# A decoder layer on one core: down biases join the sums late, gate and up biases are loaded once

## The reference

```
logits = hx @ w_router + b_router;  comb = softmax weights of the top 4 of 32
for each expert e:                       # w_gate_up[e] 1024x2048, w_down[e] 1024x1024
    gu  = hx @ w_gate_up[e] + b_gate_up[e]
    act = min(gate, 7) * sigmoid(1.702 * gate) * (clip(up, -7, 7) + 1)
    acc += comb[:, e] * (act @ w_down[e] + b_down[e])
y = LayerNorm(alpha * hx + acc) * ln2_g + ln2_b
```

## Time and profile before

| | |
|---|---|
| time, median of 3 runs | 1180.72 us (1180.72 to 1181.76) |
| the profiled execution, its own time | 1180.89 us |
| its span, first to last instruction | 1178.8 us |
| TensorE busy | 1121.9 us, 95% of the span |
| VectorE busy | 289.7 us, 25% |
| ScalarE busy | 203.8 us, 17% |
| HBM read | 450.19 MB |
| mean granted clock of TensorE | 0.990 |

### The profile page before, as it was taken

How to read it: one execution, slowest core, us unless ns; L and a number is a source line. 1 busy time by engine, 2 the same in 40 slices (tenths; PEclk the granted TensorE clock), 3 DMA queues, 4 the chain that set the end, 5 groups by cost and what they waited for, 6 DMA issues and landing times.

```text
span 1178.8 us, 14219 instructions
## 1 busy us (share of the span) xinstructions
PE 1121.9 (95%) x5374; PEld 457.7 (39%) x5375; DVE 289.7 (25%) x707; ACT 203.8 (17%) x479; POOL 30.1 (3%) x65
## 2 busy tenths in 40 slices
PE   7999999899999999999999999999999999999986
PEld 6876764533333333333332323233333333333322
DVE  1543747602121211303030303030303030303113
ACT  1322412402020202021111111111111111111111
POOL 0110111000000000000000000000000000000001
PEclk9999999899999999999999999999999999999998
DMA  9857779668999999999999999999999999999992
GB/s 361 324 197 254 269 270 384 257 263 341 423 428 427 427 428 428 429 428 428 428 428 428 428 428 428 428 427 428 429 428 428 428 428 428 428 428 428 413 424 108
DMA packets 83399, 454.21 MB, mean 385 GB/s; under 512 B 7147, under 2 KB 20099, under 8 KB 36132
## 3 DMA queue, kind: packets, MB, share of 16 engines
q1 hardware_dynamic: 80866, 440.97, 90.5%
q0 software_dynamic: 1728, 10.75, 2.5%
q10 hardware_dynamic: 770, 2.03, 0.4%
HBM read 450.19 MB, written 11.93 MB: 392 GB/s over the span
## 4 chain that ended last, share of the span: by engine, by line
PE 65%; DMA 26%; SPq 5%; ACT 2%; DVE 1%; issue 1%
DMA ring<-in_w_gate_up 23%; PE bank L1083 19%; PE bank L1125 15%; PE bank L968 5%; PE bank L664 5%; PE bank L687 5%; SPq L445 3%; PE bank L851 3%; PE bank L690 2%; DMA ring<-in_w_down 2%; PE bank L1150 2%; PE bank L964 1%; SPq L455 1%; PE bank L804 1%; ACT xtok L1313 1%; ACT actT L1313 1%
## 5 line engine op out<-in xcount | busy, mean ns | idle before, releaser
L1083 PE MATMUL bank<-ring,xg 128*64 128x512 f32 x1904 | 422.8, 597 | 23.8 <-DMA ring<-in_w_gate_up 23.8
L1083 PEld LDWEIGHTS bank<-ring,xg 128*64 128x64 f32 x1904 | 132.0, 137 | 304.8 <-issue 252.3
L1125 PE MATMUL bank<-ring,actT 128*64 128x512 f32 x960 | 215.9, 597 | 3.8 <-ACT actT L1313 3.8
L1930 DVE TENSOR_TENSOR acc<-acc,bank 128x512 f32<-128x512 f32 x60 | 41.2, 687 | 509.3 <-PE bank L1150 509.3
L1458 ACT ACTIVATE sig<-gate 128x256 f32<-128x256 f32 x64 | 26.7, 416 | 545.6 <-DVE gate L1912 545.6
L1125 PEld LDWEIGHTS bank<-ring,actT 128*64 128x64 f32 x960 | 66.6, 137 | 121.5 <-issue 118.7
L1912 DVE TENSOR_SCALAR gate<-bank 128x256 f32<-128x256 f32 x64 | 26.8, 419 | 179.0 <-PE bank L1083 157.3
L687 PE MATMUL bank<-xT,wblk 128*128 128x288 f32 x256 | 67.1, 417 | 1.4 <-DMA wblk<-in_w_in 1.4
L1450 ACT ACTIVATE xg<-bank,small 128x128 f32<-128x128 f32 x128 | 48.1, 458 | 99.1 <-PE bank L664 99.1
L968 PE MATMUL bank<-hx,pick 128*128 128x512 f32 x128 | 61.6, 626 | 0.0
L1150 PE MATMUL bank<-ybuf,spread 128*128 128x512 f32 x120 | 58.3, 618 | 0.0
(11 more groups left out here) (245 smaller groups left out, 716.8 us busy)
## 6 DMA issues: line engine op xcount, KB each, us to landing
ring<-in_w_gate_up SPq DMA_DIRECT2D x119, 2048.0 KB, 29.2
ring<-in_w_down SPq DMA_DIRECT2D x63, 2048.0 KB, 31.5
ring<-in_w_gate_up SPq DMA_DIRECT2D x16, 1024.0 KB, 18.3
wblk<-in_w_in SPq DMA_DIRECT2D x12, 1024.0 KB, 7.4
kring<-in_cache_k_moba SPq DMA_DIRECT2D x16, 256.0 KB, 5.2
vring<-in_cache_v_moba SPq DMA_DIRECT2D x16, 256.0 KB, 5.0
out<-in_state_k_win POOLq DMA_DIRECT2D x8, 512.0 KB, 4.3
out<-in_state_v_win POOLq DMA_DIRECT2D x8, 512.0 KB, 4.9
```

The lines of the kernel that those rows point to most:

```text
L1083: ins = nc.tensor.matmul(bank[n][64 * e:64 * e + 64, :], xg[:, k, 64 * e:64 * e + 64], w[:, 2048 * e + 512 * n:2048 * e + 512 * n + 512], ...
L1125: ins = nc.tensor.matmul(bank[4 + half][64 * e:64 * e + 64, :], actT[:, j, 64 * e:64 * e + 64], w[:, at:at + 512], start=(j == 0), stop=(j ...
L1930: V.tensor_tensor(o, o, new, ALU.add).then_inc(S.added, 1)
```

## The change

- The gate and up biases of all 32 experts are loaded once, in four DMAs of 32 rows, to partitions 32n to 32n+31 of `bias_rows`. For each pair VectorE makes a matrix `sel` of 32 rows (four times, one in each group of partitions) from a 32-column identity in the constants: columns of ones where row = expert. `begin_gate_up` multiplies with it, over 32 rows in place of two, and waits for it. SP's waits and loads for each pair's biases go.
- The down biases are no longer added in pair 0. In pair 14's down stage (`finish_with_biases`) TensorE turns the combination weights behind the first down unit, makes two bias products behind the second, and two more and the samples' part behind the third. They go to banks 0 to 3, which are free there. The samples' part makes first the four matmuls with the identity and then the four with `combT`. VectorE adds them to the totals before it adds pair 14's mix, and the last gate-up waits for that.
- ScalarE copies the turned weights ahead of its copies of pair 15's slots.
- `bdn` goes to partitions 64 to 96 of hx's third tile and `combT` to the same partitions beside `samp_x`, since both must live until pair 14. `acc_s` starts from zero.
- On SP the wait for the scaled sums and the load of ln2_g move ahead of unit 9 of pair 0.

```
-        def load_bias(p):
-            src = b_gate_up[0, pair_of(p), :].rearrange("e (n c) -> e n c", c=512)
-            for n in range(4):
-                sp.dma_start(bias_rows[32 * n:32 * n + 2, :], src[:, n, :]).then_inc(S.bias_in, 16)
-
-        load_bias(0)
+        for n in range(4):
+            sp.dma_start(bias_rows[E * n:E * n + E, :], b_gate_up[0, :, 512 * n:512 * n + 512]).then_inc(S.bias_in, 16)
...
-        sp.dma_start(bdn[0:E, :], b_down[0]).then_inc(S.bdn_in, 16)
-        sp.dma_start(bdn[E:E + 1, :], ln1_b[0:1, :]).then_inc(S.bdn_in, 16)
+        sp.dma_start(hx[64:64 + E, 2, :], b_down[0]).then_inc(S.bdn_in, 16)
+        sp.dma_start(hx[64 + E:65 + E, 2, :], ln1_b[0:1, :]).then_inc(S.bdn_in, 16)
...
-        def next_bias(i):
-            sp.wait_ge(S.bias_used, i + 1)
-            load_bias(i + 1)
-
+        sp.wait_ge(S.added, 5)
+        sp.dma_start(ln_g[:, :], ln2_g[0:1, :].broadcast_to([128, D])).then_inc(S.ln2_in, 16)
         load_units(0, 0, range(9, UNITS))
-        sp.wait_ge(S.sums_scaled, 6)
-        sp.dma_start(ln_g[:, :], ln2_g[0:1, :].broadcast_to([128, D])).then_inc(S.ln2_in, 16)
-        next_bias(0)
         load_units(0, 1, range(UNITS))
         with sp.Fori(1, PAIRS // 2 - 1) as m:
-            next_bias(m * 2 - 1)
             load_units(m, 0, range(UNITS))
-            next_bias(m * 2)
             load_units(m, 1, range(UNITS))
...
         def add_sample_biases():
-            pe.wait_ge(S.added, 3)
             pe.wait_ge(S.sums_scaled, 2)
+            pe.wait_ge(S.bias_added, 2)
             for q in range(4):
                 r, c = slice(NS * q, NS * q + NS), slice(256 * q, 256 * q + 256)
-                nc.tensor.matmul(bank[4][r, 0:256], ident[0:NS, 0:NS], samp_x[:, c], start=True, stop=True,
+                nc.tensor.matmul(bank[0][r, 0:256], ident[0:NS, 0:NS], samp_x[:, c], start=True, stop=True,
                                  tile_position=(0, NS * q))
-                ins = nc.tensor.matmul(bank[4][r, 256:512], combT[:, SEQ:T], bdn[:, c], start=True, stop=True,
-                                       tile_position=(0, NS * q))
-            ins.then_inc(S.spread_down, 1)
+            for q in range(4):
+                r, c = slice(NS * q, NS * q + NS), slice(256 * q, 256 * q + 256)
+                ins = nc.tensor.matmul(bank[1][r, 0:256], combT[:, SEQ:T], bdn[:, c], start=True, stop=True,
+                                       tile_position=(64, NS * q))
+            ins.then_inc(S.bias_sums, 1)
...
-            pe.wait_ge(S.bias_in, i * 64 + 64)
+            pe.wait_ge(S.bias_in, 64)
+            pe.wait_ge(S.selected, i + 1)
             for n in range(4):
-                r = slice(32 * n, 32 * n + 2)
-                ins = nc.tensor.matmul(bank[n][:, :], keep[r, C_SEL:C_SEL + 2 * SLOTS], bias_rows[r, :], start=True,
-                                       stop=False, tile_position=(32 * n, 0))
+                r = slice(E * n, E * n + E)
+                ins = nc.tensor.matmul(bank[n][:, :], sel[r, :], bias_rows[r, :], start=True, stop=False,
+                                       tile_position=(E * n, 0))
...
+        def finish_with_biases(i, m, odd):
+
+            def first_slots():
+                turn_slots(i + 1, 0)
+                turn_comb()
+
+            def other_slots():
+                pe.wait_ge(S.actT_ready, i * 2 + 2)
+                turn_slots(i + 1, 1)
+                for j in range(2):
+                    add_biases(j)
+
+            def other_biases():
+                for j in range(2, 4):
+                    add_biases(j)
+                add_sample_biases()
+
+            gather(i + 1, i * 2)
+            turn_weights(i, i * 2 + 3)
+            turn_act(i, i * 2 + 4)
+            down(i, m, odd, {0: first_slots, 1: other_slots, 2: other_biases})
...
-        gate_up(0, 0, 0, {1: turn_comb, 4: lambda: add_biases(0), 5: lambda: add_biases(1), 6: add_sample_biases})
+        gate_up(0, 0, 0)
...
         def last_gate_up(between):
 
+            pe.wait_ge(S.bias_added, 5)
             begin_gate_up(last)
...
+        def select(i, p):
+
+            if not isinstance(i, int) or i > 0:
+                dve.wait_ge(S.bias_used, i)
+            V.tensor_copy(sel[:, :].rearrange("p (e s) -> p e s", e=2),
+                          eye[:, pair_of(p)].unsqueeze(2).broadcast_to([128, 2, SLOTS])).then_inc(S.selected, 1)
...
-        start_sums()
+        select(1, 1)
         swiglu(0)
         with dve.Fori(0, PAIRS - 2) as i:
             weigh_slots(i + 1, i + 1)
             add_mixed(i)
             pick_slots(i + 2, i + 2, 0)
+            select(i + 2, i + 2)
             swiglu(i + 1)
         weigh_slots(PAIRS - 1, PAIRS - 1)
+        dve.wait_ge(S.added, 5 * PAIRS - 5)
+        add_biases()
+        dve.wait_ge(S.bias_added, 5)
         add_mixed(PAIRS - 2)
```

More of the change, by code:

```diff
@@ L44 @@
 C_ID, C_TRI, C_ONE, C_IOTA = 0, 128, 256, 384
-C_SEL = C_IOTA + CHUNKS * SLOTS
-C_HEAD = C_SEL + 2 * SLOTS
+C_EYE = C_IOTA + CHUNKS * SLOTS
+C_HEAD = C_EYE + E
 C_MEAN = C_HEAD + H
@@ L69, in constant_tables @@
     keep[:, C_ONE:C_ONE + 128] = 1
-    keep[:, C_IOTA:C_SEL] = np.arange(CHUNKS * SLOTS)
-    for n in range(4):
-        for e in range(2):
-            keep[32 * n + e, C_SEL + e * SLOTS:C_SEL + (e + 1) * SLOTS] = 1
+    keep[:, C_IOTA:C_EYE] = np.arange(CHUNKS * SLOTS)
+    keep[p, C_EYE + p % E] = 1
     keep[p, C_HEAD + p // DS % H] = 1
@@ L149, in build_layer @@
     bias_rows = place("bias_rows", [128, 512])
+    sel = place("sel", [128, 2 * SLOTS])
     share_at = cursor[0]
@@ L167, in build_layer @@
     ln_gs, ln_bs = place("ln_gs", [128, 256]), place("ln_bs", [128, 256])
+    late_at = cursor[0]
     samp_x = place("samp_x", [NS, D])
+    bdn = hx[64:64 + E + 1, 2, :]
+    combT = place("combT", [128, T], at=late_at)[64:64 + E + 1, :]
     wrt = place("wrt", [128, KC, E], at=share_at)
@@ L1188, in _ @@
         last = PAIRS - 1
-        finish(last - 1, last // 2, 0, last // 2, following=False)
+        finish_with_biases(last - 1, last // 2, 0)
         def last_gate_up(between):
+            pe.wait_ge(S.bias_added, 5)
             begin_gate_up(last)
@@ L1476, in _ @@
         take_slots(0)
-        act.wait_ge(S.comb_turned, 1)
-        copy(combT[0:E, :], bank[4][0:E, 0:T]).then_inc(S.combT_ready, 1)
         sigmoids(0)
@@ L1486, in between_pairs, with take_comb @@
             take_down(i)
+        def take_comb():
+            act.wait_ge(S.comb_turned, 1)
+            copy(combT[0:E, :], bank[3][0:E, 0:T]).then_inc(S.combT_ready, 1)
         with act.Fori(0, PAIRS - 2) as i:
@@ L1490, in _ @@
             sigmoids(i + 1)
-        between_pairs(PAIRS - 2)
+        take_gathered(PAIRS - 1)
+        take_weights(PAIRS - 2)
+        take_turned(PAIRS - 2)
+        take_comb()
+        take_slots(PAIRS - 1)
+        take_down(PAIRS - 2)
         sigmoids(PAIRS - 1, (0, 1))
@@ L1542, in _ @@
         link(V.memset(comb[:, :, :], 0.0))
-        link(V.memset(combT[E:E + 1, :], ALPHA))
         for k in range(0, KC, 2):
@@ L1857, in scale_sums @@
                     V.scalar_tensor_tensor(acc[:, t, c], hx[:, t, c], ALPHA, ln_g[:, c], ALU.mult,
-                                           ALU.mult).then_inc(S.sums_scaled, 1)
+                                           ALU.mult).then_inc(S.added, 1)
+            V.memset(acc_s[:, :], 0.0).then_inc(S.added, 1)
+            V.memset(combT[E:E + 1, :], ALPHA).then_inc(S.combT_ready, 1)
+        eye = keep[:, C_EYE:C_EYE + E]
+        def select(i, p):
[3 more added lines that the diff above has]
+                          eye[:, pair_of(p)].unsqueeze(2).broadcast_to([128, 2, SLOTS])).then_inc(S.selected, 1)
         link(V.memset(lg[:, 2, :], 0.0))
+        select(0, 0)
         router_consts()
@@ L1937, in start_sums @@
                 c = slice(512 * half, 512 * half + 512)
[L1938 to L1942, removed]
+                dve.wait_ge(S.bias_sums, j + 1)
+                V.tensor_tensor(acc[:, t, c], acc[:, t, c], bank[j][:, :], ALU.add).then_inc(S.bias_added, 1)
+            dve.wait_ge(S.bias_sums, 5)
+            link(V.tensor_tensor(acc_s[:, :], acc_s[:, :], bank[0][:, 0:256], ALU.add))
+            V.tensor_tensor(acc_s[:, :], acc_s[:, :], bank[1][:, 0:256], ALU.add).then_inc(S.bias_added, 1)
         largest_counts()
@@ L1962, in more @@
             pick_slots(i, p, c)
+            select(i, p)
             weigh_slots(i, p)
@@ L1969, in none @@
         def none(i, m, odd):
-            for sem, n in ((S.picked, 2), (S.clipped, 4), (S.dve_moe, 8), (S.act_ready, 4), (S.added, 5)):
+            for sem, n in ((S.picked, 2), (S.selected, 1), (S.clipped, 4), (S.dve_moe, 8), (S.act_ready, 4), (S.added, 5)):
                 skip(dve, sem, i, n, 5 if sem is S.added else 0)
```

43 lines of the change are left out of this document (13 added, 30 removed).

## The result

The changed kernel took 1186.76 us in the median of five runs (1182.87 to 1187.57), the kernel before 1180.72. The ratio is 1.0044, 95% interval 1.0027 to 1.0061. The forecast was 1171.0 with 1168.5 to 1175.0: the time is outside the range and on the other side. The profiled execution was the fastest of the five, 1182.87 us with a span of 1181.1; it is compared with the profiled 1180.89 and 1178.8 of before.

A forecast was written before the change was run, and what follows sets the result against it. The weight stream was taken as saturated from about 290 us, with TensorE later following it. Gains 8.7 + 3.4 - 5.5 + 3.1 = 9.7 us gave 1171.0 us, range 1168.5 to 1175.0.

The forecast's parts named there:

- front: Pair 0: gate-up without the down-bias work frees ring slots earlier and closes the weight stream's gap, gaining 8.7 us.
- middle: Pairs 2 to 14: dropping each pair's four small two-row bias loads shortens the weight stream, gaining 3.4 us.
- pair 14's last gate-up unit: The weight stream at this unit was to be 8.7 + 3.4 = 12.1 us earlier.
- pairs 14 and 15 up to the mixing: TensorE gets 5.5 us of moved work; 3.1 us of slack absorbs part, so 2.4 us come through.
- Eight units behind 263.0 without a gap end at 302.2: Weight loads from pair 0's unit 11 to pair 1's unit 7, 4.90 us each; the last landed at 310.9 before.
- my slower rival: The four 32-row bias matmuls do not overlap and take 3.8 us instead of 1.07: 1186.5 us, chance 0.03.
- SP's wait for the sums: Before ln_g's load in pair 0: ends near 232.8 us, before the first free slot at 244.35, so costs nothing.
- The end: Pair 14: down-bias and sample work moved there adds 5.5 us to TensorE, of which 2.4 come through.
- The terms of the work: Moved work in pair 14: turning the weights 0.46, four bias products 3.82, samples 1.3 us.
- The clock: Danger named: the forecast fails if the clock between 225 and 240 us, ahead of the first slot, comes out otherwise.

The follow-up runs named there:

- a_ring512: The changed kernel with 384 bytes of padding ahead of the ring, so that every weight slot starts at a multiple of 512 bytes: 1169.87 us.
- d_late: The kernel before with only the down biases moved to pair 14 and ln_g's load moved earlier, slots at multiples of 512 bytes: 1172.01 us.
- c_once: The kernel before with only the gate and up biases loaded once and picked by `sel`, slots at multiples of 512 bytes: 1174.64 us.
- after_again: The changed kernel run once more, nothing altered: 1183.13 us in ten runs, ratio 1.0032 to the kernel before.
- h_two: c_once plus four unread loads a pair, each two rows of 2 KB, where the bias loads stood: 1178.66 us.
- h_spread: c_once plus four unread loads a pair, each 16 rows of 256 bytes, where the bias loads stood: 1176.97 us.
- e_pair12: a_ring512 with the down biases added in pair 12's down stage instead of pair 14's: 1167.18 us.
- g_rows32: The kernel before with bias matmuls reading 32 rows in place of two, 30 of them zeros, the bias tile cleared once at the start: 1177.30 us.
- b_ring128: The kernel before with 128 bytes of padding ahead of the ring and nothing else changed: 1194.01 us.

## Why the prediction was wrong

In microseconds, the profiles of before and of a_ring512, which is the change with the address put back:

| step | predicted | measured | from |
|---|---|---|---|
| front | 8.7 | 8.5 | d_late |
| middle | 3.4 | 3.1 | 13 x (59.04 - 58.80), c_once's period |
| earlier start of the stream, by the clock | not in the sum | 2.5 | first unit starts 3.49 earlier and takes 6.36 instead of 5.35 |
| pair 14's last gate-up unit | 12.1 | 14.1 | 1078.46 - 1064.37 |
| pairs 14 and 15 up to the mixing | -2.4 | -1.1 | 86.41 against 85.29 |
| stop ahead of the small product | 0 | -3.1 | 18.1 against 15.05 from the mixing on |
| sum | 9.7 | 9.9 | spans 1178.8 and 1168.9 |
| address of the ring | not in the sum | -12.2 | spans 1168.9 and 1181.1 |

The first gate-up unit of a_ring512, for the third row:

```profile
232.08 6.36 PE L1063 MATMUL bank<-first,xg 128*64 128x512 f32 x16 [2.56 <-ACT xg L1453]
```

- **The step that failed** is that the unit's 4.90 us, read from the kernel before, was carried over to the kernel after. "Eight units behind 263.0 without a gap end at 302.2", and the middle with it, take a load to cost what it did. The full diff had shown otherwise: it resizes the constants and places `sel` ahead of the ring. I cost `sel` by VectorE's time alone. The shift costs 0.84 us a pair, 12.4 us at pair 14's last gate-up unit (1076.79 - 1064.37).
- **What the table leaves out.** It is made from profiled executions. The median of the changed kernel, 1186.76, is 3.9 us above its profiled 1182.87, so of the 15.8 us by which 1171.0 was missed the address explains 12.2. The units at the lower clock in after_again are a part of the rest; all of it was not traced.
- **Slower, but not by my slower rival.** Its 1186.5 lies beside the measured 1186.76 by luck. That one had the 32-row matmuls in series. They take 1.07 us, as costed. SP's wait for the sums ended at 233.8, as costed.
- **Front and middle** were right in mechanism and in size. d_late has the one alone. For the middle, h_two and h_spread show that loads on few engines stretch the period more than the same bytes over sixteen.
- **The end.** The terms of the work were right (0.45, 3.82, and 1.13 for the samples against 1.3). That 2.4 of it comes through was not: e_pair12, without it in pair 14, needs 86.94 us from pair 14's last gate-up unit to the mixing, a_ring512 with it 86.41. There the work fills time in which TensorE would have waited for the last pair's loads. Those loads take longer than before: from pair 14's last gate-up unit to pair 15's first down unit, which waits for its load in all three, it is 66.78 us in c_once and 67.66 in e_pair12, against 65.87 before. Two-row loads seem to go with the shorter times, since g_rows32 and h_two, which have them, take 65.79 and 64.78, and h_spread takes 67.89. Why was not tried.
- **The clock** came out otherwise, as I had named it as a danger, and in the good direction. g_rows32 shows that the 32-row matmuls do it.
- **The stop** was not foreseen. It cost 2.5 us of the changed kernel's span and 3.1 of a_ring512's. It stands in all six profiles of kernels that have both parts with the down biases in pair 14, and in none of the others: before, b_ring128, c_once, d_late, e_pair12, g_rows32, h_two and h_spread. Where it comes from stays open; sixteen empty instructions do not move it.
- The near match of 9.7 and 9.9 is partly luck: 2.5 us of clock, which no term had, stand against 3.1 of the stop, and the end cost 1.3 less than forecast.

## What to carry to other kernels

A tile that is added or resized moves everything placed behind it: before the durations of an old trace are used for a new kernel, compare the start addresses of what the DMA engines write, and keep the large ones at multiples of 256 bytes. When a stream is the bound, find the first moment from which it runs without a gap, and charge loads of few rows not by bytes but by the busiest engine that they fall on. An edit on the faster engine counts only where the stream waits for it: some 10 us of work taken out of pair 0 were worth 8.5, and 5.4 us put into pair 14 cost nothing.

## What the runs showed of the hardware

- A load whose rows start 64 or 128 bytes past a multiple of 256 in SBUF runs 1.4% slower with runs of 8 KB (4.97 against 4.90 us for 2 MB), whichever of the two it is, and about 3% slower with runs of 4 KB (408 against 422 GB/s); at 256 past a multiple of 512 it is as fast as at a multiple of 512.
- Four small loads with two rows of 2 KB in a stream of 24 MB stretch it by 0.39 us, the same 16 KB in rows of 256 bytes over 16 rows by 0.08 (periods of 59.19, 58.88 and, without them, 58.80 us).
- Four bias matmuls with 32 rows, 30 of them zeros, kept the granted clock of the next 5 us at 1.00 where those with two rows left it at 0.50 (0.76 in d_late), at the same 1.07 us.
- TensorE can stand still for 3 us between the first weight load of a small product and the rest of it, with no wait that the profile shows (2.95 to 3.62 us in six profiles), in one arrangement of a kernel and not in another with the same work (e_pair12).
